# Three expert slots at 96 tokens in unrounded float32, in two and four column tiles, in place of 128 tokens in split precision

## The chip, the cores and the metric

One core of one Trainium2 chip runs the whole program in one launch. The metric is the device time of that launch in microseconds (us), lower is better. Three runs of the kernel before gave 1510.27, 1510.45 and 1510.76 us, median 1510.45. TensorE is called PE here, its weight loads PEld, VectorE DVE, ScalarE ACT, GpSimd POOL, SyncE SP.

## What is computed

A two-layer encoder over 256 tokens of width 1024. Each layer has three mixing branches (a gated MLP, latent attention, differential attention), and then a feed-forward part: dense in layer 0, a mixture of experts in layer 1. Only the mixture is touched:

```python
def swiglu(h, w1, w3, w2):
    return (jax.nn.silu(h @ w1) * (h @ w3)) @ w2

def moe_ffn(h, router, w1, w3, w2):
    logits = (h @ router).astype(jnp.float32)
    top_v, top_i = lax.top_k(logits, TOP_K)          # 2 of 8
    top_w = jax.nn.softmax(top_v, axis=-1)
    gates = jnp.sum(jax.nn.one_hot(top_i, N_EXPERTS, dtype=jnp.float32) * top_w[..., None], axis=-2)
    y = gates[..., 0:1] * swiglu(h, w1[0], w3[0], w2[0])
    for e in range(1, N_EXPERTS):
        y = y + gates[..., e:e + 1] * swiglu(h, w1[e], w3[e], w2[e])
    return y
```

There are 8 experts, each with w1 and w3 of 1024x3584 and w2 of 3584x1024 in float32, 44 MB an expert. Evaluated with its own inputs, the reference's router sends 38 tokens to expert 0 and 97, 73, 45, 64, 66, 54 and 75 to experts 1 to 7 (512 places in all).

## The kernel before

**Stages.** Layer 0, layer 1's mixer, the router, and then the experts, one *slot* after the other. SP loads each expert in 42 units of 1 MB (128 partitions x 2048 floats) into a ring of 14 buffers (`eraw`). It loads a unit as soon as the matmuls on the unit 14 places before it are done (`eunit_done`). PE works on the units in the order of the table `ORDER`, which for the four column blocks (`PAIRS`) of the hidden layer holds the units of w1, w3 and w2. A unit has two k-steps of 128 rows x 1024 columns; the four units of w1 and w3 of the last, half as wide block have four k-steps of 128 x 512. That makes 92 k-steps in a slot: 76 of 1024 columns and 16 of 512.

**Slots.** `PLAN = "WLWWL"` gives the kinds of slots 0 to 4. Slot 0 is always expert 0. Experts 1 to 7 are ranked by their number of tokens; the three with the fewest take the light slots (1, 4 and the last, 7), the others the wide ones. A slot that is needed because an expert has more tokens than its slot has room is put in behind slot 6.

- A *wide* slot (W, 128 tokens, function `slot`) works in split precision. ACT rounds the weights (`ehi <- eraw`, `unit_hi`), DVE makes the rest (`elo <- eraw, ehi`, `unit_lo`), and PE multiplies three times for each 512 columns: high by high (L2001), high weights by low tokens (L2002), low weights by high tokens (L2006).
- A *light* slot (L, 64 tokens, `light_slot`) multiplies the loaded float32 weights as they are (L2533). The stationary tokens are 64 wide, so PE's array is used as two column tiles: one matmul computes the left half of the columns for output partitions 0 to 63, the next one the right half for partitions 64 to 127. In the trace each such float32 matmul is two records.

**Around a slot.** After w1 and w3 of a block, ACT takes silu, DVE the product into `hid`, and PE transposes `hid` at fixed units (`TURNS`); at unit 31 PE also gathers the next slot's tokens. The reads of the units are waited for on `eraw_in`.

**Ahead of slot 0.** PE finishes the last mixer units (`token_pair`), with the transposes of the first 128 tokens in between (`tokens_turned(0)`), computes the router's logits with the router's 8 columns as the stationary operand (`logits`, L2205), transposes the second 128 tokens, computes their logits, and places the tokens (L2413 to L2417). DVE builds the selection matrix `Gm`; PE gathers expert 0's tokens with it (L2553), ACT and DVE split them (`hehi`, `helo`), and slot 0 begins.

Of the kernel before, what the change touches and what calls it, by code (L numbers as in the profile page):

```python
# [43 lines left out]


SLOT = P
EXTRA = 2 * TOKENS // (SLOT + 1)
SLOTS = NE + EXTRA
MORE = -(-TOKENS // SLOT) - 1
NM = NE * MORE  # L50
assert MORE == 1

PLAN = "WLWWL"
LIGHT, CAP = PLAN.count("L") + 1, 64
RANKED = NE - 1
LOOP = len(PLAN)
assert PLAN[0] == "W"


def is_light(s):
    return PLAN[s] == "L"


def lights_before(s):
    return PLAN[:s].count("L")


def wides_before(s):  # L70

    return s - (lights_before(s) if isinstance(s, int) else LIGHT - 1)


def slot_row(s):

    if isinstance(s, int) and s < LOOP:
        if is_light(s):
            return SLOT + CAP * lights_before(s)
        return SLOT * wides_before(s) + (CAP * (LIGHT - 1) if s else 0)  # L80
    return s * SLOT - (SLOT - CAP) * (LIGHT - 1)
# [5 lines left out]
def rank_of_slot(s):  # L87
    return lights_before(s) if s < LOOP and is_light(s) else LIGHT + wides_before(s) - 1
# [80 lines left out]
T_LOW = T_IOTA + SLOT  # L169
T_THR = T_LOW + NE * NE  # L170
T_EID = T_THR + NM
T_TRIM = T_EID + NM
T_IDX = T_TRIM + NM * NM
T_COS = T_IDX + EXTRA
T_SIN = T_COS + NB * ROPE // 2
T_W = T_SIN + NB * ROPE // 2
# [59 lines left out]
def encoder(nc, ins, out):  # L236
    ctx = ExitStack()
    with ctx:
# [46 lines left out]
        rt = keep("rt", [P, KD, NE])  # L285
# [98 lines left out]
        ea32 = at("ea32", over_mask, [P, 8, CAP])  # L384
        last32 = at("last32", over_xn + 4096, [P, 4, CAP])
# [3 lines left out]
        lgT = keep("lgT", [NE, TOKENS])  # L389
# [16 lines left out]
        qm = keep("qm", [P, NB, NE])  # L406
        tmp = keep("tmp", [P, EXTRA, NM])
        tmp2 = keep("tmp2", [P, 2, NB, EXTRA, NM])
# [12 lines left out]
        he32 = keep("he32", [P, KD, CAP])  # L421
# [106 lines left out]
        first_hehi = sem("first_hehi")  # L528
# [42 lines left out]
        xs_all = nc.dram_tensor("xs_all", [slot_row(SLOTS) + SLOT, D], F32, kind="Internal")  # L571
# [59 lines left out]
        def light_tiles(p):  # L631

            return last32 if p == PAIRS - 1 else ea32

# [76 lines left out]
        def _(pool):  # L711
# [31 lines left out]
            pool.dma_start(rt[:, :, :], ins["moe_router"][0].rearrange("(k p) e -> p k e", p=P)).then_inc(router_in, 16)  # L743
# [21 lines left out]
            for i in range(TABLE_BLOCKS):  # L765
                pool.wait_ge(unit_done, MIX_UNITS + 6 + 3 * i // 2)
                r = min(SLOT * i, slot_row(SLOTS))
                pool.dma_start(xs_all[r:r + SLOT, :], zeros[:, :]).then_inc(zeroed, 16)
# [22 lines left out]
            def slot_in(s):  # L791
                if isinstance(s, int) and s in DIRECT:
                    return
                n = CAP if isinstance(s, int) and s < LOOP and is_light(s) else SLOT
                pool.dma_start(xs[0:n, :], xs_all[bass.ds(slot_row(s), n), :]).then_inc(xs_in, 16)
# [20 lines left out]
            for s in range(1, LOOP + 1):  # L816
                result_waited(s)
                if not is_light(s - 1):
# [5 lines left out]
                pool.wait_ge(y_left, 16 * lights_before(s))  # L824
# [38 lines left out]
        def turned_place(b, k):  # L863

            return small[:, 2 * b + k // 4, P * (k % 4):P * (k % 4) + P]

        def first_place(k):
# [3 lines left out]
            return t[:, SLOT * (k % 2):SLOT * (k % 2) + SLOT]  # L873

# [9 lines left out]
        def _(act):  # L884
# [233 lines left out]
            def outputs(s):  # L1118

                act.wait_ge(eunit_done, UNITS * s + UNITS)  # L1120
                if isinstance(s, int) and is_light(s):
                    act.activation(ysb[:, 0:512], small[:, 0, :], ACT.Copy).then_inc(y_ready, 1)
# [9 lines left out]
            def slot(s, first=False):  # L1132
                for n in range(UNITS):
# [6 lines left out]
                    if first and n == 5:  # L1140

                        act.wait_ge(lmax_ready, 1)
                        for b in range(NB):
                            i = act.activation(ex[:, b, :], lg[:, b, :], ACT.Exp, bias=lmax[:, b:b + 1],
                                               scale=nrs[:, 3, b:b + 1])
                        i.then_inc(lexp_ready, 1)
# [20 lines left out]
                    if n == GATES_TURNED + 2 and first:  # L1167

                        act.wait_ge(gt_done, 1)
                        act.activation(GT[:, :, :].rearrange("j b t -> j (b t)"), small[0:SLOT, 2, 0:NB * P],  # L1170
                                       ACT.Copy).then_inc(gt_ready, 1)
                    if n in HE_TAKEN and not (isinstance(s, int) and is_light(s + 1)):
# [4 lines left out]
            def light_slot(s, i, final=False):  # L1177
                for n in range(UNITS):
                    if n == 3:
# [3 lines left out]
                    for p in range(PAIRS):  # L1183
                        if n == unit_end(p, 0):

                            act.wait_ge(eunit_done, UNITS * s + n + 1)
                            if p:
                                act.wait_ge(light_turned, PAIRS * i + p)
                            act.activation(hid[:, 0:light_width(p)], big[0][:, 0, 0:light_width(p)],
                                           ACT.Silu).then_inc(sil_done, 1)  # L1190
                        if n == TURNS[2 * p]:

                            act.wait_ge(light_turned, PAIRS * i + p + 1)
                            tiles = light_width(p) // P
                            src = small[:, turn_bank(2 * p), 0:2 * tiles * CAP].rearrange("p (j h t) -> p j h t", j=tiles, h=2)
                            dst = light_tiles(p)[:, 0:2 * tiles, :].rearrange("p (h j) t -> p j h t", h=2)
                            act.activation(dst, src, ACT.Copy).then_inc(light_taken, 1)
                    if n in HE_TAKEN and not final and not (s + 1 < LOOP and is_light(s + 1)):
# [7 lines left out]
            unit_hi(0, 0)  # L1206
# [5 lines left out]
            def squares(b):  # L1212
                for half in range(2):
                    act.wait_ge(x_ready, 8 + 2 * b + half + 1)
                    part = slice(512 * half, 512 * half + 512)
                    i = act.activation(xn[:, b, part], X[:, b, part], ACT.Square, accum_out=nss[:, 3, half, b:b + 1])
                return i

            def tokens_taken(b):
                act.wait_ge(norm_turned, 12 + 2 * b + 1)  # L1220
                for k in range(4):
# [3 lines left out]
            squares(0)  # L1225
            tokens_taken(0)
            tokens_taken(1)
            squares(1).then_inc(ss_ready, 1)
            act.wait_ge(var_ready, 4)
            act.activation(nsd[:, 3, :], nvar[:, 3, :], ACT.Sqrt, scale=1.0 / D, bias=eps[:, :]).then_inc(sd_ready, 1)  # L1230
            act.wait_ge(unit_done, NU - 2)
            unit_hi(0, 1)
# [4 lines left out]
            for k in range(KD):  # L1237
                act.wait_ge(first_gather, k // 2 + 1)
                a = act.activation(hehi[:, k, :], first_place(k), ACT.Copy, scale=pcol[:, G_ROUTE + k:G_ROUTE + k + 1])
                if k % 2:  # L1240
                    a.then_inc(first_hehi, 1)
            slot(0, first=True)
            for s in range(1, LOOP):
                if is_light(s):
                    light_slot(s, lights_before(s))
# [6 lines left out]
            light_slot(last, LIGHT - 1, final=True)  # L1252
# [27 lines left out]
        def _(dve):  # L1280
# [125 lines left out]
            def mixer(l):  # L1406
# [220 lines left out]
                if l:  # L1627
# [6 lines left out]
                    dve.memset(room[:, 0:1], float(SLOT))  # L1634
# [14 lines left out]
                def tokens_taken(b):  # L1649
                    dve.wait_ge(norm_turned, 12 + 2 * b + 2)  # L1650
                    for k in range(4, KD):
# [9 lines left out]
                else:  # L1661

                    unit_lo(0, 0)
# [3 lines left out]
                    tokens_taken(0)  # L1667
                    add(1, G_O + 1)
                    tokens_taken(1)
# [51 lines left out]
            dve.tensor_copy(lgT[:, :], big[0][0:NE, 0, 0:TOKENS]).then_inc(lgt_ready, 1)  # L1721
# [19 lines left out]
            own(dve.tensor_scalar(qS[:, :, 0:NE], pos[:, :, :], -1.0, None, ALU.add))  # L1741
# [3 lines left out]
            def picked():  # L1745

                for b in range(NB):
                    i = dve.tensor_scalar(Gm[:, b, :], iota, qS[:, b, 0:1], nrs[:, 3, b:b + 1], ALU.is_equal, ALU.mult)
                i.then_inc(g_ready, 1)

# [15 lines left out]
            def gathered(s, i):  # L1766

                dve.wait_ge(hehi_ready, 2 * (wides_before(s) - 1) + i + 1)
# [17 lines left out]
            def ranked():  # L1786
# [11 lines left out]
                dve.tensor_scalar(room[:, 1:NE], place_of[:, :], float(LIGHT), float(CAP - SLOT), ALU.is_lt, ALU.mult)  # L1798
# [9 lines left out]
            def extra_slots():  # L1808


                own(dve.tensor_tensor(need[:, :], counts[:, :], room[:, :], ALU.is_gt))
# [17 lines left out]
            def extra_places():  # L1829
                for b in range(NB):  # L1830
                    i = dve.tensor_tensor(qm[:, b, :], qS[:, b, 0:NE], room[:, :], ALU.subtract)
                own(i)
                for j, part in enumerate((qm[:, :, :], gS[:, :, 0:NE])):
                    for b in range(NB):
                        i = dve.tensor_tensor(tmp2[:, j, b, :, :], pick[:, :, :], bc(part[:, b, :], 1, [P, EXTRA, NM]), ALU.mult)
                own(i)
                dve.tensor_reduce(qS[:, :, NE:SLOTS], tmp2[:, 0, :, :, :], AX.X, ALU.add)
                own(dve.tensor_reduce(gS[:, :, NE:SLOTS], tmp2[:, 1, :, :, :], AX.X, ALU.add))
                dve.tensor_copy(metai[:, :], meta[:, :]).then_inc(routed, 1)

            def destinations():
# [8 lines left out]
                dve.tensor_scalar(shift[:, :], idx[:, :], float(SLOT), float(slot_row(NE - 1)), ALU.mult, ALU.add)  # L1850
# [5 lines left out]
                own(dve.tensor_tensor(over[:, :, :], over[:, :, :], placed[:, :, :], ALU.add))  # L1856
                for c in range(2):
# [11 lines left out]
            unit_lo(0, 1)  # L1869
# [782 lines left out]
```

## Time and profile before

| | us |
|---|---|
| median of three runs | 1510.45 |
| the profiled execution | 1509.97 |
| its span, first to last instruction | 1508.3 |
| slot 0 (W), first matmul to that of slot 1 | 119.45 |
| slot 1 (L), to the first matmul of slot 2 | 81.94 |
| slot 2 (W) | 119.93 |
| slot 3 (W) | 118.46 |
| slot 4 (L) | 82.45 |

TensorE's granted clock is 0.999 of 2.4 GHz over the span. In a profile, a record of PE has its start and a modelled end; matmuls overlap, so the pace of the engine is the distance from start to start, not the length of a record.

### The profile page before, as it was taken

Reading aid. Unit: us, or ns where it says so; the run is one execution under the profiler, and the core shown is the slowest. Engines: PE = TensorE matmul, PEld = TensorE weight load, DVE = VectorE, ACT = ScalarE, POOL = GpSimd, SP = SyncE. Lnnn points to the kernel's source line nnn. Section 1 sums busy time; section 2 is a strip of 40 time slices with the busy share of each in tenths; the row PEclk is TensorE's granted clock in tenths of the full one; section 3 lists DMA queues with packets and bytes.
Section 4 is the critical chain, followed back from the end, with each engine's and each line's share of the span. In section 5 each row is a group of like instructions: output and inputs, shape, how many; then the busy total and the mean of one; then the engine's idle time right before and its main releaser. Section 6 shows DMA issues by size and latency. Waiting matters only on the chain.

```text
span 1508.3 us, 19634 instructions
## 1 busy us (share of the span) xinstructions
PE 1481.6 (98%) x7704; PEld 1146.8 (76%) x7704; DVE 967.4 (64%) x899; ACT 794.3 (53%) x787; POOL 98.2 (7%) x101
## 2 busy tenths in 40 slices
PE   9999999999999999999999999999999999999996
PEld 8888889999898888878853588888734688888532
DVE  6856776455467667689930399898700798998301
ACT  5465635343354655487720387777501786877201
POOL 2000000000000000002000000200000000200041
PEclk9999999999999999999999999999999999999999
DMA  9555455778575554899999999999999999999996
GB/s 338 197 168 175 147 186 177 232 257 249 186 256 168 168 171 151 325 389 382 406 390 427 426 427 427 424 421 427 390 411 427 427 426 427 427 428 408 388 426 282
DMA packets 111772, 488.65 MB, mean 324 GB/s; under 512 B 8492, under 2 KB 12720, under 8 KB 68688
## 3 DMA queue, kind: packets, MB, share of 16 engines
q1 hardware_dynamic: 103520, 459.58, 78.3%
q0 software_dynamic: 7600, 27.37, 4.9%
q8 instruction: 57, 0.93, 0.2%
q10 hardware_dynamic: 576, 0.61, 0.1%
q14 instruction: 19, 0.16, 0.0%
HBM read 473.37 MB, written 15.21 MB: 324 GB/s over the span
## 4 chain that ended last, share of the span: by engine, by line
PE 87%; DMA 6%; DVE 3%; SPq 2%; ACT 2%; issue 1%; DVEq 0%; ACTq 0%
PE big L2001 15%; PE big L2006 15%; PE big L2002 14%; PE big L2533 7%; DMA eraw<-experts 6%; PE small L2006 6%; PE small L2001 5%; PE small L2002 5%; PE big L2078 4%; PE big L2085 4%; PE big L2079 4%; PE small L2106 3%; SPq L696 2%; DVE elo L1393 2%; PE small L2533 1%; ACT ehi L1108 1%
## 5 line engine op out<-in xcount | busy, mean ns | idle before, releaser
L1393 DVE TENSOR_TENSOR elo<-eraw,ehi 128x2048 fp32r<-128x2048 f32 x210 | 476.0, 2289 | 69.9 <-ACT ehi L1108 68.1
L1108 ACT ACTIVATE ehi<-eraw 128x2048 fp32r<-128x2048 f32 x210 | 401.3, 1919 | 149.3 <-PE big L2006 64.4
L1297 DVE TENSOR_TENSOR wlo<-raw,whi 128x2048 fp32r<-128x2048 f32 (+2 forms) x104 | 229.9, 2217 | 140.9 <-ACT whi L895 140.0
L895 ACT ACTIVATE whi<-raw 128x2048 fp32r<-128x2048 f32 (+2 forms) x103 | 190.6, 1857 | 223.3 <-PE big L2006 83.3
L2001 PE MATMUL big<-ehi,hehi 128*128 128x512 f32 x560 | 219.9, 393 | 5.3 <-ACT ehi L1108 5.2
L2002 PE MATMUL big<-ehi,helo 128*128 128x512 f32 x560 | 218.1, 389 | 0.0
L2001 PE MATMUL big<-whi,hhi 128*128 128x512 f32 (+1 forms) x384 | 151.9, 396 | 0.0
L2006 PE MATMUL big<-elo,hehi 128*128 128x512 f32 x560 | 150.3, 390 | 0.8 <-DVE elo L1393 0.8
L2533 PE MATMUL big<-eraw,he 128*64 128x512 f32 (+1 forms) x768 | 147.6, 541 | 2.7 <-DMA eraw<-experts 2.7
L2002 PE MATMUL big<-whi,hlo 128*128 128x512 f32 (+1 forms) x384 | 149.0, 388 | 0.0
L1952 DVE TENSOR_TENSOR hid<-hid,big 128x512 f32<-128x512 f32 (+1 forms) x12 | 7.5, 622 | 206.6 <-PE big L2533 206.6
L2001 PEld LDWEIGHTS big<-ehi,hehi 128*128 128x128 f32 x560 | 105.2, 188 | 29.2 <-ACT ehi L1108 4.6
L2006 PEld LDWEIGHTS big<-elo,hehi 128*128 128x128 f32 x560 | 104.8, 188 | 24.2 <-DVE elo L1393 2.5
L2533 PEld LDWEIGHTS big<-eraw,he 128*64 128x64 f32 x768 | 54.0, 137 | 89.4 <-issue 80.7
L2002 PEld LDWEIGHTS big<-ehi,helo 128*128 128x128 f32 x560 | 105.2, 188 | 21.3
L2078 PE MATMUL big<-hhi,whi 128*128 128x256 f32 x480 | 117.4, 285 | 0.9 <-DVE hlo L1307 0.7
L2079 PE MATMUL big<-hlo,whi 128*128 128x256 f32 x480 | 116.7, 283 | 0.0
L2006 PE MATMUL big<-wlo,hhi 128*128 128x512 f32 (+1 forms) x384 | 94.9, 387 | 0.0
L2001 PE MATMUL small<-ehi,eahi 128*128 128x512 f32 x240 | 94.0, 391 | 0.0
L2078 PEld LDWEIGHTS big<-hhi,whi 128*128 128x128 f32 x480 | 92.0, 192 | 1.9 <-issue 1.1
L2002 PE MATMUL small<-ehi,ealo 128*128 128x512 f32 x240 | 93.4, 389 | 0.0
L2079 PEld LDWEIGHTS big<-hlo,whi 128*128 128x128 f32 x480 | 92.1, 192 | 0.2
(405 smaller groups left out, 1855.7 us busy)
## 6 DMA issues: line engine op xcount, KB each, us to landing
eraw<-experts SPq DMA_DIRECT2D x336, 1024.0 KB, 16.9
raw<-ffn_w SPq DMA_DIRECT2D x30, 1024.0 KB, 5.8
raw<-w_gate SPq DMA_DIRECT2D x24, 1024.0 KB, 5.0
raw<-w_in SPq DMA_DIRECT2D x19, 1024.0 KB, 5.1
raw<-w_branch SPq DMA_DIRECT2D x12, 1024.0 KB, 5.0
raw<-w_o SPq DMA_DIRECT2D x8, 1024.0 KB, 5.0
xs_all<-zeros POOLq DMA_DIRECT2D x11, 512.0 KB, 7.0
raw<-w_in SPq DMA_DIRECT2D x4, 896.0 KB, 9.2
```

The costliest lines, as they stand in the source:

```text
L895: act.activation(whi[u % HI][:, 0:kt, 0:cols], raw[u % RAW][:, 0:kt, 0:cols], ACT.Copy).then_inc(hi_ready, 1)
L1108: act.activation(ehi[HI_OF[n]][:, :], eraw[n % RING][:, :], ACT.Copy).then_inc(ehi_ready, 1)
L1297: dve.tensor_tensor(wlo[u % RAW][:, 0:kt, 0:cols], raw[u % RAW][:, 0:kt, 0:cols], whi[u % HI][:, 0:kt, 0:cols].bitcast(F32), ALU.subtract) ...
L1393: dve.tensor_tensor(elo[n % RING][:, :], eraw[n % RING][:, :], ehi[HI_OF[n]][:, :].bitcast(F32), ALU.subtract).then_inc(elo_ready, 1)
L2001: pe.matmul(o, sh, mh, start=start, stop=False, **kw)
L2002: return pe.matmul(o, sl, mh, start=False, stop=False, **kw)
L2006: return pe.matmul(o, sh, ml, start=False, stop=stop, **kw)
L2078: pe.matmul(place(n), w_of, ahi[:, k0 + k, :], start=start, stop=False, skip_group_check=True)
L2079: pe.matmul(place(n), w_of, alo[:, k0 + k, :], start=False, stop=False, skip_group_check=True)
L2085: i = pe.matmul(place(n), wlo[u % RAW][:, k, n * P:n * P + P], ahi[:, k0 + k, :], start=False, stop=last and k == kt - 1, skip_group_check ...
L2106: return pe.transpose(o, src, ident[0:n, 0:n])
L2533: d = pe.matmul(out[CAP * side:CAP * side + CAP, 0:cols], x32[:, t, :], raw32[:, k, cols * side:cols * side + cols], start=start, stop=stop)
```

## The change

`PLAN` becomes `"MLMML"`. A *medium* slot (M) has room for 96 tokens and works on unrounded float32 as a light slot does: tokens 0 to 63 in two column tiles of 64, as before, and after them, in the same k-step, tokens 64 to 95 in four column tiles of 32, each with a quarter of the columns. Slots 0, 2 and 3 are medium; expert 0 takes slot 0, and of the ranked experts the fourth and fifth lightest take slots 2 and 3. The two fullest take the wide slots 5 and 6. Slots 1, 4 and the last stay light. In M slots ACT's and DVE's conversions of the weights (`unit_hi`, `unit_lo`) are gone, and so is the split of the tokens; silu and product work on 768 columns instead of 1024 (128 partitions). A medium slot writes its result in six transfers instead of one.

```diff
-PLAN = "WLWWL"
-LIGHT, CAP = PLAN.count("L") + 1, 64
+PLAN = "MLMML"
+CAP, MID = 64, 96
+LIGHT = PLAN.count("L") + 1
+MEDIUM = PLAN[1:].count("M")
...
                     def products(k, stop):
                         t = tiles * q + k
                         start = t == 0 and (m < 2 or p == 0)
+                        shared = medium and cols < 512
                         for side in range(2):
-                            d = pe.matmul(out[CAP * side:CAP * side + CAP, 0:cols], x32[:, t, :],
-                                          raw32[:, k, cols * side:cols * side + cols], start=start, stop=stop)
+                            d = pe.matmul(out[CAP * side:CAP * side + CAP, 0:cols], x32[:, t, 0:CAP],
+                                          raw32[:, k, cols * side:cols * side + cols], start=start, stop=stop, skip_group_check=shared)
+                        if medium:
+                            w = cols // 2
+                            for j in range(TILES):
+                                d = pe.matmul(out[COLS * j:COLS * j + COLS, cols:cols + w], x32[:, t, CAP:MID],
+                                              raw32[:, k, w * j:w * j + w], start=start and not shared, stop=stop,
+                                              skip_group_check=shared)
                         return d
...
                             for j in range(w // P):
                                 d = turn(small[:, turn_bank(2 * p), P * j:P * j + P], hid[:, P * j:P * j + P])
+                            if medium:
+                                at = 0 if p < PAIRS - 1 else w
+                                for j in range(w // P // 2):
+                                    d = turn(small[:, 3, at + P * j:at + P * j + P], hid[:, w + P * j:w + P * j + P])
```

The router is changed too. Its matrix is padded to 32 columns and its eight products rotate over four column tiles; the four partial sums are added by the small matmul that had been the transpose of `lgT`. Half of the second 128 tokens are transposed inside the last mixer unit, and their read-out is shared out anew between ACT and DVE:

```diff
-                    i = pe.matmul(big[0][0:NE, 0, P * b:P * b + P], rt[:, k, :], hT[:, k, P * b:P * b + P], start=k == 0,
-                                  stop=k == KD - 1)
+                    rows = slice(COLS * (k % TILES), COLS * (k % TILES) + COLS)
+                    i = pe.matmul(big[0][rows, 0, P * b:P * b + P], rt[:, k, :], hT[:, k, P * b:P * b + P], start=k < TILES,
+                                  stop=k >= KD - TILES)
...
-            logits(0)
-            tokens_turned(1)
-            logits(1).then_inc(logits_done, 1)
+            logits(0, range(KD))
+            logits(1, range(4))
+            tokens_turned(1, (range(4, KD),))
+            logits(1, range(4, KD)).then_inc(logits_done, 1)
```

On PE, ahead of slot 0, from the last mixer product to the first matmul of the token placement, there stood before (rows read: line, operation, output<-inputs, stationary columns x moving columns, count):

```order
L2006 MATMUL big<-wlo_78,hhi 128x512 x4
L2205 MATMUL big<-hT,rt 8x128 x8
L2106 MATMUL small<-tab,X 128x128 x8
L2205 MATMUL big<-hT,rt 8x128 x8
L2123 MATMUL small<-tab 128x128
L2106 MATMUL small<-tab,lgT 128x8 x2
```

and there stands now (the first row is the first half of the transposes, ahead of the last four products of the mixer):

```order
L2166 MATMUL small<-tab,X 128x128 x4
L2064 MATMUL big<-wlo_78,hhi 128x512 x4
L2269 MATMUL big<-hT,rt 32x128 x12
L2166 MATMUL small<-tab,X 128x128 x4
L2269 MATMUL big<-hT,rt 32x128 x4
L2183 MATMUL small<-tab 128x128
L2473 MATMUL small<-tab,lgT 128x8 x2
```

Four of the eight transposes moved ahead of the mixer's last products, and four of the second tokens' eight products moved ahead of the other four transposes.

On PE, the first unit of slot 0 and what is ahead of it, before (L2553 is the gather, `he` the tokens, `eraw_142` the first ring buffer):

```order
L2553 MATMUL big<-Gm,X 128x128 x4
L2001 MATMUL big<-ehi_138,hehi 128x512
L2002 MATMUL big<-ehi_138,helo 128x512
L2001 MATMUL big<-ehi_138,hehi 128x512
L2002 MATMUL big<-ehi_138,helo 128x512
L2001 MATMUL big<-ehi_138,hehi 128x512
L2002 MATMUL big<-ehi_138,helo 128x512
L2001 MATMUL big<-ehi_138,hehi 128x512
L2002 MATMUL big<-ehi_138,helo 128x512
L2006 MATMUL big<-elo_156,hehi 128x512 x4
```

and now, with the second unit behind it:

```order
L2649 MATMUL big<-Gm,X 128x96 x4
L2609 MATMUL big<-eraw_142,he_179 64x512 x2
L2614 MATMUL big<-eraw_142,he_179 32x256 x4
L2609 MATMUL big<-eraw_142,he_179 64x512 x2
L2614 MATMUL big<-eraw_142,he_179 32x256 x4
L2609 MATMUL big<-eraw_143,he_179 64x512 x2
L2614 MATMUL big<-eraw_143,he_179 32x256 x4
L2609 MATMUL big<-eraw_143,he_179 64x512 x2
L2614 MATMUL big<-eraw_143,he_179 32x256 x4
```

A unit of 12 matmuls, all 128 wide, became one of 12 float32 matmuls whose width goes from 64 to 32 and back in each k-step.

## Rows read from the trace of the kernel before

**Rows 1.** The page: busy times, granted clock by slice, chain that ended last.

```profile
PE 1481.6 (98%) x7704; PEld 1146.8 (76%) x7704; DVE 967.4 (64%) x899; ACT 794.3 (53%) x787; POOL 98.2 (7%) x101
...
PEclk9999999999999999999999999999999999999999
...
PE 87%; DMA 6%; DVE 3%; SPq 2%; ACT 2%; issue 1%; DVEq 0%; ACTq 0%
```

**Rows 2.** Windows, slots 0 to 4: length, busy us, PEclk, DMA share, GB/s.

```profile
652.05:771.50 119.45, 119.23 (x547) 98.08 (x547) 109.16 (x125) 86.05 (x59) 14.20 (x9) 1.00 0.97 387
771.50:853.44 81.94, 79.01 (x416) 31.02 (x415) 4.76 (x13) 9.36 (x18) 1.55 (x4) 1.00 1.01 420
853.44:973.37 119.93, 119.33 (x541) 98.22 (x542) 107.60 (x63) 90.89 (x63) 7.37 (x4) 1.00 1.01 426
973.37:1091.83 118.46, 118.46 (x543) 97.98 (x543) 102.34 (x58) 83.53 (x52) 6.79 (x5) 1.00 1.00 412
1091.83:1174.28 82.45, 79.04 (x415) 31.01 (x415) 4.67 (x13) 9.36 (x18) 1.51 (x4) 1.00 1.00 419
```

**Rows 3.** PE's timeline in slot 1: around the first transposes of `hid`, and w3's units.

```profile
788.65 1.89 PE L2533 MATMUL big<-eraw,he 128*64 128x512 f32 x8
790.47 0.66 PE L2106 MATMUL small<-tab,hid 128*128 128x128 f32 x4
791.05 1.94 PE L2533 MATMUL big<-eraw,he 128*64 128x512 f32 x8
...
816.73 4.46 PE L2533 MATMUL big<-eraw,he 128*64 128x512 f32 x20
```

**Rows 4.** PE's timeline in slot 1, later transposes, and the gather behind them.

```profile
827.99 0.66 PE L2106 MATMUL small<-tab,hid 128*128 128x128 f32 x4
828.48 2.73 PE L2498 MATMUL big<-Gm,X 128*128 128x128 f32 x23
```

**Rows 5.** PE's timeline in slot 1, units with 256 moving columns.

```profile
832.15 7.13 PE L2533 MATMUL big<-eraw,he 128*64 128x256 f32 x64
```

**Rows 6.** PE's timeline, from the last mixer products into the router.

```profile
637.51 0.39 PE L2002 MATMUL big<-whi,hlo 128*128 128x512 f32 x1
637.74 1.08 PE L2006 MATMUL big<-wlo,hhi 128*128 128x512 f32 x4
638.75 1.91 PE L2205 MATMUL big<-hT,rt 128*8 128x128 f32 x16
640.60 1.09 PE L2106 MATMUL small<-tab,X 128*128 128x128 f32 x8
```

**Rows 7.** The timeline of all engines, router to first gather.

```profile
638.86 0.69 DVE L1647 TENSOR_TENSOR X<-X,big 128x512 f32<-128x512 f32 x1 [1.64 <-PE big L2006]
...
641.71 2.04 PE L2205 MATMUL big<-hT,rt 128*8 128x128 f32 x16
641.73 1.13 DVE L1652 TENSOR_SCALAR hT<-small,pcol 128x128 f32<-128x128 f32 x4 [2.18 <-PE small L2106]
...
643.78 0.41 DVE L1721 COPY lgT<-big 8x256 f32<-8x256 f32 x1
...
647.59 0.17 DVE L1741 TENSOR_SCALAR qS<-pos 128x16 f32<-128x16 f32 x1
```

**Rows 8.** PE's timeline, first gather and first matmul of slot 0.

```profile
651.24 1.06 PE L2553 MATMUL big<-Gm,X 128*128 128x128 f32 x8
652.05 0.47 PE L2001 MATMUL big<-ehi,hehi 128*128 128x512 f32 x1
```

**Rows 9.** PE's timeline, from slot 1 into slot 2.

```profile
849.04 1.94 PE L2533 MATMUL small<-eraw,last 128*64 128x512 f32 x8 [0.48 <-DMA eraw<-experts]
853.44 0.47 PE L2001 MATMUL big<-ehi,hehi 128*128 128x512 f32 x1 [2.46 <-ACT ehi L1108]
```

**Rows 10.** The chain that ended last, from slot 1 into slot 2.

```profile
825.94 29.17 DMA eraw<-experts
855.13 1.92 ACT ehi L1108
857.08 2.30 DVE elo L1393
```

**Rows 11.** PE's timeline, the last unit of slot 4.

```profile
1169.78 1.94 PE L2533 MATMUL small<-eraw,last 128*64 128x512 f32 x8 [0.56 <-DMA eraw<-experts]
```

**Rows 12.** DMA issues: operation and count, KB each, median us to landing.

```profile
eraw<-experts SPq DMA_DIRECT2D x336, 1024.0 KB, 16.9
```

More of the change, by code:

```diff
@@ L633, in light_tiles, with native_width @@
             return last32 if p == PAIRS - 1 else ea32
+        def native_width(p, medium):
+            return light_width(p) * 3 // 2 if medium else light_width(p)
         def light_width(p):
@@ L1140, in slot @@
                     if first and n == 5:
[L1142 to L1146, printed above, removed]
+                        expert_weights()
                     if not first or n >= EARLY:
@@ L1235, in _ @@
                 act.activation(xn[:, b, :], X[:, b, :], ACT.Copy, scale=nrs[:, 3, b:b + 1]).then_inc(xn_ready[b], 1)
[L1237 to L1242, printed above, removed]
+            light_slot(0, 0, first=True)
             for s in range(1, LOOP):
-                if is_light(s):
-                    light_slot(s, lights_before(s))
+                if is_native(s):
+                    light_slot(s, natives_before(s))
                 else:
@@ L1827, in extra_slots, with slots_known @@
                                       float(slot_row(SLOTS) - SLOT * SLOTS), ALU.mult, ALU.add))
[L1829 to L1838, printed above, removed]
+            def slots_known():
                 dve.tensor_copy(metai[:, :], meta[:, :]).then_inc(routed, 1)
@@ L1958, in light_slot @@
                         (light_gathered if to_light else gathered)(s + 1, HE_TAKEN.index(n))
-            slot(0, first=True)
+            light_slot(0, first=True)
             for s in range(1, LOOP):
-                (light_slot if is_light(s) else slot)(s)
+                (light_slot if is_native(s) else slot)(s)
             dve.wait_ge(routed, 1)
@@ L2052, in token_pair @@
                                       whi[u % HI][:, k, 0:cols], False)
+                        if b and half:
+                            late()
                         pe.wait_ge(lo_ready, u + 1)
@@ L2487, in slot @@
                     if n == GATHERED:
-                        gather(s + 1, CAP if isinstance(s, int) and is_light(s + 1) else SLOT)
+                        gather(s + 1, capacity(s + 1) if isinstance(s, int) else SLOT)
             def gather(s, rows):
@@ L2506, in gather, with gates_turned, light_slot @@
                     i.then_inc(gather_done, 1)
-            def light_slot(s, i, final=False):
+            def gates_turned():
+                pe.wait_ge(gg_ready, 1)
+                for b in range(NB):
+                    i = turn(small[0:SLOT, 2, b * P:b * P + P], Gg[:, b, :])
+                i.then_inc(gt_done, 1)
+            def light_slot(s, i, final=False, first=False):
+                medium = not final and is_medium(s)
                 for n in range(UNITS):
                     p, m, q = ORDER[n]
-                    if n == 0:
+                    if first and n < 4:
+                        pe.wait_ge(first_he, n + 1)
+                    elif n == 0:
                         pe.wait_ge(he_ready, 2 * s)
@@ L2539, in light_slot @@
                     d.then_inc(eunit_done, 1)
+                    if n == GATES_TURNED and first:
+                        pe.wait_ge(light_taken, 2)
+                        gates_turned()
                     for p in range(PAIRS):
```

326 lines of the change are left out of this document (196 added, 130 removed).

## The prediction

> **What bounds the kernel now.** I read the page first: PE is busy 98% of the span at full clock and makes up 87% of the chain that ended last [rows 1]. Then the windows by slot. In the three wide slots that change, PE is busy 119.23 of 119.45, 119.33 of 119.93 and 118.46 of 118.46 us; DVE (102 to 109 us) and ACT (84 to 91 us) are close behind but do not hold it. At the same time the DMA engines are at a share of 0.97 to 1.01 and move 387 to 426 GB/s [rows 2]. So there are two bounds near each other, PE in wide slots and the loads in light ones: slot 1 ends with PE waiting for a landing [rows 9], and the chain holds a piece of 29.17 us that is a load [rows 10]. What the change is worth is decided by one question: how long PE needs for a medium slot, against some 119 us.
>
> **Pace of PE in float32.** I read it from spans of many records, not from record lengths. In slot 1 twenty records, ten passes of the tile pair, span 4.46 us and eight span 1.89 [rows 3]: six passes more in 2.57, so a pass takes 0.43 us for 512 columns (0.429), both tiles of a pair run side by side in it, and the last one ends 0.60 after its start. With 256 columns 64 records (32 passes) span 7.13, so a pass takes 0.215 us [rows 5]. Transposes with 128 columns follow each other at 0.11 [rows 4, 6]. So a pass costs its columns at 0.84 ns each, and a float32 matmul is two passes.
>
> **A k-step of a medium slot.** 64 tokens: two passes of 512, 0.86 us. 32 tokens: the four tiles each take 256 columns; if they run side by side as the pairs do, two passes of 256, 0.43 us. Together 1.29; in the half-wide block 0.645. A slot has 76 of the first and 16 of the second: 97.9 + 10.3 = 108.2 us. To this come the transposes, 6 + 6 + 6 + 3 of `hid` and 8 of the gather at 0.11, 3.2 us. Without anything else a medium slot would be some 111.4 us, 7 below a wide one. It has the same number of column passes as the wide one and gains only in pace.
>
> **The change of tile width.** This is the term that decides. In rows 3 the four passes that start at 788.65 are streamed at 788.65 + 4 x 0.429 = 790.37, but the first 128-wide transpose starts at 790.47, 0.10 later; then four transposes span 0.66 where 3 x 0.11 + 0.27 = 0.60 would do, 0.05 more. Going back, the transposes are streamed at 790.96 and the 64-wide matmul starts at 791.05, 0.09 later, and its eight records span 1.94 instead of 1.89, another 0.05. So a change of width costs 0.15 us to 128 and 0.145 us to 64. It is not the transposes and not the wait in front of them: transposes followed by a 128-wide gather start 0.49 us apart for four, at their usual pace with no gap behind [rows 4]. The router shows it a third time: the four 128-wide products, 0.23 apart, are streamed at 637.74 + 4 x 0.23 = 638.66, and the 8-wide matmul starts at 638.75, some 0.10 later with nothing more behind (16 records in 1.91 = 15 x 0.109 + 0.27, the length of a single one); on the way back 0.10 and 0.05 [rows 6].
>
> A medium slot changes width twice in each of its 92 k-steps, from 64 to 32 and back. No row shows that very change. Its bounds are 0 (the gap belongs only to changes between the whole array and tiles) and 0.15 each. I take the rows' value, as all four directions that the trace has show at least 0.10: 0.145 to 64, and to 32 between the 0.10 of 8 columns and the 0.145 of 64, 0.115. That is 0.26 per k-step, S below. The Trainium skill ("TensorEngine Tiling (Array Packing)", Tiling Modes, Key Properties) says that changing the tiling mode, not just the tile, drains TensorE, and lists 128x64 and 128x32 as different modes; by it the rows' gap would be paid here too, 92 times two. The trace agrees for 128 to 64, 128 to 8 and back. A sum that counted only passes, as that page's speedup table does, would give 1490 instead of the figure below.
>
> So M = 108.2 + 3.2 + 92 x 0.26 + 0.6 (each of the four groups of transposes adds one change) = **135.9 us** for a medium slot; in general 112.0 + 92 S.
>
> **The sum.**
> - *Start of slot 0.* Today the X half lands at 639.55 (DVE, 638.86 + 0.69), but PE first does 16 router records and transposes from 640.60; the second products start at 641.71 and DVE copies the logits at 643.78 [rows 6, 7]. Afterwards four transposes (0.45) come earlier and delay the half to 640.0; meanwhile twelve products run in four tiles, 3 x 2 passes of 0.11, 0.65 us. The other four transposes take 0.6, read-out two per engine 0.28 each (four in 1.13) with about 0.2 to start, then one group of four products, 0.5 with its tail: copy at about 641.8, 2.0 earlier. The step on `qS` (0.17) moves behind `Gm` [rows 7]. I take 2.2 us; the gather still ends it [rows 8]. Bounds 0 and 3.
> - *Slot 0:* -2.2 + 135.9 - 119.45 = **+14.3** [rows 2].
> - *Slot 1* stays: same code, starts with a full ring.
> - *Slot 2:* slot 1's last unit is done at about 849.04 + 1.94 = 850.98 [rows 9]; today slot 2 is through at 973.37, 122.39 later, since its first units go from landing over ACT and DVE to PE [rows 9, 10]. A medium slot starts on the landed unit; its second lands at 855.11 (825.94 + 29.17), so it is held by about 1.0. 1.0 + 135.9 - 122.39 = **+14.5**.
> - *Slot 3:* 135.9 - 118.46 = **+17.4** [rows 2].
> - *Slots 4 to 7* stay: slot 4 starts with a full ring as today.
> - *At nothing:* ACT and DVE conversions of three slots, up to 109 us of DVE a slot. They lay beside PE's work; their absence shortens nothing but the start of slot 2. The 768-column silu and product and the second read-out of transposes fall on engines that are now nearly idle, with two or more units of PE's work between a transpose and its use. The six result transfers instead of one are on POOL, and the copy that waits for them comes a slot later. DMA: fewer bytes per us are asked for than today, so it is no bound in M slots.
>
> Sum +46.2. The profiled execution took 1509.97 (span 1508.3, 1.7 around it), 0.5 below the median of the runs: **1556 us**.
>
> **What would decide it otherwise.** The total is 3 M - 361.5, zero at M = 120.5, S = 0.092, 46 ns a change. With S = 0.20 (0.10 each) it is +29.7, 1540; with S = 0.30 +57.3, 1567.
>
> **Rivals.**
> 1. *Changes between 64 and 32 cost nothing; faster.* For it: the rows only show changes that include 128 or an 8-wide tile. Against it: the 8-wide matmul is also a tile of the array, and it paid both ways [rows 6]. Then M = 112.6 (108.2 + 3.2 + four groups of transposes at 0.29). Slot 0 gives -2.2 - 6.9 = -9.0. Slots 2 and 3 would give -8.8 - 5.9 = -14.7, but now the loads bind: slots 2 to 4 need 126 units, at 426 GB/s 2.46 us each for 1.049 MB [rows 2, 12], 310.1 us, and took 320.7 (850.98 to 1171.72) [rows 9, 11], so at most -10.6. Sum -19.6: **1490**. It decides from 46 ns a change downward. Chance 0.20, with 0.03 for a partial cost that ends within 0.2% (S about 0.08 to 0.10) and 0.02 for one that ends between 1490 and 1507.
> 2. *The four tiles of 32 don't run side by side*, four float32 streams at once being more than any row shows (pairs at most). Then the 32 tokens cost 4 x 0.43 instead of 0.43 a k-step: 76 x 1.29 + 16 x 0.645 = 108 us more a slot, about **1880**. The Trainium skill ("TensorE: Matmul & The Clock Gate", Part 3) gives 2.38 times for three column tiles of 32 and some 4 ns for each further tile; no run here shows it. Chance 0.04.
> 3. *A ninth slot*, some 118 us [rows 2], if 96 are too few for an expert in an M slot: excluded by the counts, 38 for expert 0 and 66 and 73 for the fourth and fifth lightest; the loads show that today's 8 slots (336 units of 42) suffice [rows 12].
>
> **How the numbers follow.** Width changes paid as in the rows: 0.71, of which its own range is 1540 to 1567. Serial tiles 0.04, faster 0.22, within 0.2% 0.03. 0.2% (3 us) is about what a measurement of this kernel can tell from no change. The range must take in the faster case, else it leaves out more than 0.2: 1487 to 1569, the bounds of the two large cases with 2 or 3 us for the start. Chances: faster 0.22, same 0.03, slower 0.75.
>
> **What the profile after would show.** PE in a medium slot: passes of 0.43 and 0.215, and between the last 32-wide pass and the next 64-wide record 0.09 to 0.10 of gap, with 0.05 more behind it, in each of 92 k-steps. Slot 0 some 136 long and starting near 649.9; slots 2 and 3 136 to 137; slots 1 and 4 still near 82; in M slots the loads near 42 x 1.049 MB in 136 us, 324 GB/s, with the queue waiting for PE. If instead k-steps start every 1.29 us, rival 1 holds and light slots get longer; if the four 32-wide records start 0.2 apart, rival 2. ACT and DVE should be idle for most of M slots without anyone gaining.

## The result, and the profile after

The changed kernel takes 1566.28 us (median of 4 runs, 1566.0 to 1567.3), the kernel before beside it 1510.36 (1509.29 to 1510.76). The ratio is 1.0373, 95% interval 1.0361 to 1.0386: slower by 55.9 us, where 46 was forecast. The profiled execution took 1567.3 us with a span of 1565.7, 57.4 above the span before.

The page after, its lines of busy times and of the chain (against [rows 1]):

```profile
PE 1539.7 (98%) x9485; PEld 959.4 (61%) x9485; DVE 665.8 (43%) x735; ACT 547.5 (35%) x642; POOL 87.7 (6%) x120
...
PE 91%; DMA 6%; SPq 1%; ACT 1%; DVE 1%; issue 0%; DVEq 0%; ACTq 0%
```

DVE and ACT lost 302 and 247 us of work, and PE's work did not get shorter for it. Windows of the profile after, slots 0 to 4 (columns as in [rows 2]; slot 1 and slot 4 end here with their last matmul):

```profile
652.41:791.28 138.87, 138.87 (x1136) 35.65 (x1136) 15.06 (x76) 6.76 (x14) 5.32 (x9) 1.00 0.92 340
791.28:872.08 80.80, 79.08 (x418) 31.06 (x414) 3.41 (x6) 5.17 (x9) 4.05 (x9) 1.00 1.01 414
872.08:1011.09 139.01, 138.52 (x1133) 35.63 (x1133) 4.35 (x6) 6.69 (x13) 2.00 (x5) 1.00 0.99 404
1011.09:1149.59 138.50, 138.50 (x1137) 35.46 (x1133) 4.93 (x10) 6.90 (x13) 3.43 (x8) 1.00 0.89 322
1149.59:1228.26 78.67, 78.67 (x418) 31.03 (x414) 4.64 (x12) 7.23 (x17) 3.99 (x9) 1.00 1.00 419
```

A medium slot takes 138.5 to 139.0 us where a wide one took 118.5 to 119.9 [rows 2], with PE busy throughout, and the loads fall to 322 GB/s once they only follow PE. Why it is that long stands in PE's timeline in slot 0, two k-steps:

```profile
700.57 1.08 PE L2609 MATMUL big<-eraw,he 128*64 128x512 f32 x4
701.58 0.64 PE L2614 MATMUL big<-eraw,he 128*32 128x256 f32 x8
702.15 1.08 PE L2609 MATMUL big<-eraw,he 128*64 128x512 f32 x4
703.16 0.64 PE L2614 MATMUL big<-eraw,he 128*32 128x256 f32 x8
```

A k-step is 702.15 - 700.57 = 1.58 us, where its passes are 1.29. From 64 to 32 wide the start is 1.01 away, for 0.86 of passes; from 32 to 64 it is 0.57, for 0.43. So the pair of changes costs 0.29. The eight 32-wide records span 0.64: two passes of 0.215 and the tail, so four tiles do run side by side (one after the other, eight records would take 1.7).

Where the 57.4 us of span came from, slot by slot (slot 0 from its first matmul, a light slot to its last):

| | before | after | difference | forecast |
|---|---|---|---|---|
| first matmul of slot 0 | 652.05 | 652.41 | +0.4 | -2.2 |
| slot 0 | 119.45 | 138.87 | +19.4 | +16.5 |
| slot 1 | 79.48 | 80.80 | +1.3 | 0 |
| slot 2, from the end of slot 1 | 122.39 | 139.01 | +16.6 | +14.5 |
| slot 3 | 118.46 | 138.50 | +20.0 | +17.4 |
| slot 4 | 79.87 | 78.67 | -1.2 | 0 |
| the rest | | | +0.8 | 0 |

### The profile page after: what moved, and what is told of

Same layout as the page of the kernel before. It is cut to its first block, busy times and chain, and to the rows that moved or that the text cites. A ratio compares the mean times of both kernels' runs of the same rounds, so it can differ in the third digit from the quotient of the medians.

```text
span 1565.7 us, 22782 instructions
## 1 busy us (share of the span) xinstructions
PE 1539.7 (98%) x9485; PEld 959.4 (61%) x9485; DVE 665.8 (43%) x735; ACT 547.5 (35%) x642; POOL 87.7 (6%) x120
## 3 DMA queue, kind: packets, MB, share of 16 engines
q8 instruction: 71, 1.16, 0.3%
## 4 chain that ended last, share of the span: by engine, by line
PE 91%; DMA 6%; SPq 1%; ACT 1%; DVE 1%; issue 0%; DVEq 0%; ACTq 0%
PE big L2609 18%; PE big L2059 10%; PE big L2060 10%; PE big L2064 10%; PE small L2609 7%; PE big L2614 6%; DMA eraw<-experts 5%; PE big L2138 4%; PE big L2145 4%; PE big L2139 4%; PE small L2614 3%; PE small L2059 3%; PE small L2060 3%; PE small L2064 3%; PE small L2166 3%; SPq L720 1%
## 5 line engine op out<-in xcount | busy, mean ns | idle before, releaser
L2609 PE MATMUL big<-eraw,he 128*64 128x512 f32 (+1 forms) x1536 | 334.3, 553 | 3.1 <-DMA eraw<-experts 3.1
L930 ACT ACTIVATE whi<-raw 128x2048 fp32r<-128x2048 f32 (+2 forms) x103 | 190.6, 1857 | 225.9 <-PE big L2064 79.9
L1439 DVE TENSOR_TENSOR elo<-eraw,ehi 128x2048 fp32r<-128x2048 f32 x84 | 190.7, 2289 | 30.9 <-ACT ehi L1143 30.1
L2609 PEld LDWEIGHTS big<-eraw,he 128*64 128x64 f32 x1536 | 92.0, 136 | 157.1 <-issue 148.4
L1143 ACT ACTIVATE ehi<-eraw 128x2048 fp32r<-128x2048 f32 x84 | 160.9, 1920 | 61.2 <-PE big L2064 25.8
L2609 PE MATMUL small<-eraw,ea 128*64 128x512 f32 x576 | 142.8, 606 | 3.4 <-DMA eraw<-experts 3.3
L2614 PE MATMUL big<-eraw,he 128*32 128x256 f32 (+1 forms) x1536 | 112.5, 364 | 0.0
L2059 PE MATMUL big<-ehi,hehi 128*128 128x512 f32 x224 | 88.5, 395 | 2.5 <-ACT ehi L1143 2.5
L2060 PE MATMUL big<-ehi,helo 128*128 128x512 f32 x224 | 88.1, 393 | 0.0
L2059 PEld LDWEIGHTS big<-whi,hhi 128*128 128x128 f32 x384 | 72.1, 188 | 16.9 <-issue 3.3
L2060 PEld LDWEIGHTS big<-whi,hlo 128*128 128x128 f32 x384 | 72.2, 188 | 14.1 <-issue 0.5
```

Of the source, the lines that this page charges most:

```text
L930: act.activation(whi[u % HI][:, 0:kt, 0:cols], raw[u % RAW][:, 0:kt, 0:cols], ACT.Copy).then_inc(hi_ready, 1)
L1143: act.activation(ehi[HI_OF[n]][:, :], eraw[n % RING][:, :], ACT.Copy).then_inc(ehi_ready, 1)
L1439: dve.tensor_tensor(elo[n % RING][:, :], eraw[n % RING][:, :], ehi[HI_OF[n]][:, :].bitcast(F32), ALU.subtract).then_inc(elo_ready, 1)
L2059: pe.matmul(o, sh, mh, start=start, stop=False, **kw)
L2060: return pe.matmul(o, sl, mh, start=False, stop=False, **kw)
L2609: d = pe.matmul(out[CAP * side:CAP * side + CAP, 0:cols], x32[:, t, 0:CAP], raw32[:, k, cols * side:cols * side + cols], start=start, stop ...
```

## The experiments

The kernel before was run beside each group of them, at medians of 1510.95, 1510.21 and 1509.89 us. Ratios are to it.

**1. Fewer width changes, same work** (`e1_unit`, `e2_snake`, `e3_snake2`). The two widths of a k-step become two passes over a unit (`part(n, width)` does all its k-steps at one width); then units alternate which width comes first; then groups of two units do so:

```diff
...
-                    for k in range(tiles):
-                        d = products(k, k == tiles - 1 and (n == UNITS - 1 or (m < 2 and tiles * q + k == KD - 1)))
-                    d.then_inc(eunit_done, 1)
...
+                        if not SNAKE or any(ORDER[n][0] == PAIRS - 1 and ORDER[n][1] < 2 and ORDER[n][2] == 0 for n in ns):
+                            width = CAP
+                        for n in ns:
+                            arrive(n)
+                            part(n, width)
+                        width = CAP + COLS - width
+                        for n in ns:
+                            part(n, width).then_inc(eunit_done, 1)
...
```

> Same work as the changed kernel, but in a medium slot the 64-wide matmuls of all k-steps of a unit come first and then the 32-wide ones: 42 pairs of width changes in a slot instead of 92. Theory (a width change costs 0.1455 us, half of the 0.291 per k-step read in the changed kernel): 50 x 0.291 = 14.6 us less per medium slot, slot about 124.3, total about 1522.6. Rival A (the 32-wide matmuls themselves are slow, however they are ordered): no change, 1566. Rival B (loads or waits hold the slot): no change either.

> As the one before, but every second unit starts with the width at which the last one ended, so that a unit has one width change: 42 changes in a slot instead of 184. Theory: 142 x 0.1455 = 20.7 us less per medium slot than in the changed kernel, slot about 118, total about 1504, which is below the kernel before. Rival A: 1566.

> As the one before, but in groups of two units: 22 width changes in a slot. Theory: 162 x 0.1455 = 23.6 us less per medium slot than in the changed kernel, slot about 115.2, total about 1496. Rival A: 1566. Rival C (once PE is this fast, the loads hold the end of slot 4): 1 to 5 us above that, seen as waits for landings in slot 4.

Measured: 1523.11 us (1.0084, 1.0067 to 1.0101), 1508.29 (0.9984, 0.9975 to 0.9994) and 1508.17 (0.9984, 0.9974 to 0.9993). The order of the same matmuls is worth 58 us, so rivals A and B of the expectations are out. Slot 3 of each, from the windows of the three profiles in this order:

```profile
982.78:1106.86 124.08, 124.08 (x1137) 44.57 (x1134) 4.93 (x10) 6.90 (x13) 3.42 (x8) 1.00 0.98 385
```

```profile
970.90:1089.52 118.62, 118.62 (x1135) 48.15 (x1133) 4.93 (x10) 6.91 (x13) 3.43 (x8) 1.00 1.01 416
```

```profile
968.38:1084.12 115.74, 115.74 (x1135) 50.05 (x1133) 4.94 (x10) 6.80 (x13) 3.43 (x8) 1.00 1.01 425
```

With 184, 84, 42 and 22 changes between 64 and 32 the slot takes 138.5, 124.1, 118.6 and 115.7 us, PE busy in all of it: 0.144, 0.131 and 0.145 us a change from one to the next. The uneven step comes from what is not counted: where the width is the same on both sides of a group of 128-wide transposes, the group adds two changes and not one. Counted in the order of `ORDER` and `TURNS` with those changes in, a slot has 187, 87, 50 and 30, and the price is 0.144, 0.148 and 0.144. On to none, 115.7 - 30 x 0.145 = 111.4, what passes and transposes alone add up to in the prediction (108.2 + 3.2). The slots came out as the theory says (124.3, 118, 115.2), and so did the first total (1522.6). The other two totals are 4 and 12 us above it. In the windows of the third, the light slots are 83.3 long, where the kernel before has 79.5 and 79.9:

```profile
767.47:850.72 83.25, 79.58 (x416) 31.10 (x412) 3.42 (x6) 5.17 (x9) 4.05 (x9) 1.00 1.01 418
...
1084.12:1167.41 83.29, 80.04 (x416) 31.05 (x412) 4.64 (x12) 7.23 (x17) 3.99 (x9) 1.00 1.01 423
```

and PE's timeline at the end of its slot 4 shows the last units of w2 waited for one by one, and then slot 5's first weights:

```profile
1158.16 1.94 PE L2614 MATMUL small<-eraw,ea 128*64 128x512 f32 x8 [0.19 <-DMA eraw<-experts]
1160.60 1.94 PE L2614 MATMUL small<-eraw,ea 128*64 128x512 f32 x8 [0.51 <-DMA eraw<-experts]
1163.02 1.94 PE L2614 MATMUL small<-eraw,last 128*64 128x512 f32 x8 [0.48 <-DMA eraw<-experts]
1165.47 1.94 PE L2614 MATMUL small<-eraw,last 128*64 128x512 f32 x8 [0.52 <-DMA eraw<-experts]
1170.67 0.80 PE L2060 MATMUL big<-ehi,hehi 128*128 128x512 f32 x1 [3.27 <-ACT ehi L1144]
```

**2. Half of each load left out** (`e8_snake2_half`), to see whether that is the whole of it:

```diff
-                    sp.dma_start(eraw[n % RING][:, :], src).then_inc(eraw_in[n % RING], 16)
+                    part = slice(0, 1024 if half or (first and n >= RING) else 2048)
+                    sp.dma_start(eraw[n % RING][:, part], src[:, part]).then_inc(eraw_in[n % RING], 16)
```

> The kernel with 22 width changes in a medium slot (groups of two units, 1508.2 us where 1496 was expected), with half of each unit's load left out in slots 0 to 4 once the ring is full (those experts compute with stale halves). If the loads took back the missing 12 us: slots 1 and 4 fall to 78.7 (from 83.3 both), slots 0, 2 and 3 stay at 115.5 to 116.3, and slot 5 starts without waiting for a landing, total about 1491. If PE itself (wrongly priced width changes) is the cause: unchanged, 1508.

Measured: 1490.81 us (0.9872, 0.9852 to 0.9892). Its windows:

```profile
652.27:768.77 116.50, 116.50 (x1137) 50.43 (x1137) 15.07 (x76) 6.66 (x14) 5.32 (x9) 1.00 0.66 220
768.77:847.19 78.42, 78.42 (x417) 31.16 (x415) 3.42 (x6) 5.16 (x9) 4.04 (x9) 1.00 0.85 282
847.19:962.96 115.77, 115.77 (x1136) 50.19 (x1134) 4.35 (x6) 6.58 (x13) 1.99 (x5) 1.00 0.61 202
962.96:1078.70 115.74, 115.74 (x1135) 50.05 (x1133) 4.93 (x10) 6.80 (x13) 3.42 (x8) 1.00 0.60 195
1078.70:1157.25 78.55, 78.55 (x417) 31.01 (x413) 6.02 (x13) 10.55 (x19) 3.98 (x9) 1.00 0.92 331
```

The medium slots keep their PE time (slot 2 is without its 1.4 us of waits), the light slots are at 78.4 and 78.6, and PE waits for nothing in these five slots. So full loads cost the kernel of 22 changes 17 us: 11.3 in slots 0 to 4, the rest behind them, where slot 5's start waits 3.3 us in the one kernel and not in the other. That is more than the 12 us missed above, since the kernel before waits for loads too (at the ends of its light slots and the starts of slots 2 and 5 [rows 9, 11]); how much it would gain from half loads was not measured.

**3. No width change in the k-steps** (`e5_all32`). All 96 tokens go into 32-wide tiles, three groups a k-step, and the hidden layer's and the results' layout follow (light slots keep their products):

```diff
...
-                        for side in range(2):
-                            d = pe.matmul(out[CAP * side:CAP * side + CAP, 0:cols], x32[:, t, 0:CAP],
-                                          raw32[:, k, cols * side:cols * side + cols], start=start, stop=stop, skip_group_check=shared)
-                        if medium:
-                            w = cols // 2
...
+                        w = cols // 2
+                        for g in range(MID // COLS):
                             for j in range(TILES):
-                                d = pe.matmul(out[COLS * j:COLS * j + COLS, cols:cols + w], x32[:, t, CAP:MID],
-                                              raw32[:, k, w * j:w * j + w], start=start and not shared, stop=stop,
-                                              skip_group_check=shared)
+                                d = pe.matmul(out[COLS * j:COLS * j + COLS, w * g:w * g + w], x32[:, t, COLS * g:COLS * g + COLS],
+                                              raw32[:, k, w * j:w * j + w], start=start and w * g % 512 == 0, stop=stop,
+                                              skip_group_check=True)
...
```

> Medium slots with all 96 tokens in four column tiles of 32, three groups a k-step: the same passes as in the changed kernel and no width change except around the transposes. Theory (only passes and width changes cost PE anything): 1.29 us a k-step, a slot of about 112.5 us. For the total two theories differ. PE alone decides: three slots at 112.5 give about 1490. The loads hold the light slots (in the two runs with few width changes the last unit of slot 3 landed at the same 1060.7 us as in the kernel before): slot 4 cannot end before some 1164, total about 1503. Rival (24 matmuls a k-step, four float32 streams at once, are more than PE can be fed with): a slot well over 113.

Measured: 1510.58 us (0.9999, 0.999 to 1.0008), as the kernel before; neither 1490 nor 1503. Its slots 0, 2 and 3 take 116.88, 118.30 and 118.28, not 112.5. In PE's timeline of slot 2 the passes keep their pace, and between them stand gaps that no semaphore ended; in slot 3 the 128 records behind such a gap span 5.37 us instead of 3.70, of which more below:

```profile
939.79 3.68 PE L2621 MATMUL big<-eraw,he 128*32 128x128 f32 x128
944.95 3.70 PE L2621 MATMUL big<-eraw,he 128*32 128x128 f32 x128 [1.48 <-issue]
950.88 1.74 PE L2621 MATMUL big<-eraw,he 128*32 128x128 f32 x56 [2.24 <-issue]
...
1065.16 5.37 PE L2621 MATMUL big<-eraw,he 128*32 128x128 f32 x128 [2.22 <-issue]
1071.22 5.39 PE L2621 MATMUL small<-eraw,ea 128*32 128x256 f32 x96 [0.69 <-issue]
```

The view of PE's waits for slots 0 to 3 sums them:

```profile
PE big L2621 <- issue: 8.3, 5, 2.2
PE small L2615 <- DMA eraw<-experts: 2.3, 2, 1.1
PE small L2621 <- issue: 0.9, 2, 0.7
PE big L2621 <- DMA eraw<-experts: 0.5, 1, 0.5
```

Of the gaps without a releaser, 9.2 us in seven, the five of the first row (8.3) stand in the half-wide block, whose k-steps of 0.645 us have 12 matmuls, which are 24 records, with as many weight loads (the 24 of the expectation are records). The other two stand right behind that block.

**4. The same with half of each load left out** (`e7_half`, the edit of 2 on the kernel of 3).

> As the one before, but the loads of slots 0 to 4 bring only half of each unit once the ring has been filled (the other half is stale data, so these experts compute something else; passes, waits and order stay). If the loads hold the kernel before it, light slots fall to their PE time of 78.7, slot 4 ends near 1146 and the total is about 1485, some 18 us below its sibling with full loads. If PE alone decides there, the two are equal.

Measured: 1484.76 us (0.9839, 0.9824 to 0.9854). Slots 0, 2 and 3 now take 113.88, 113.03 and 114.30, and the view of PE's waits for the same stretch has one row:

```profile
PE small L2624 <- issue: 1.0, 1, 1.0
```

So full loads cost this kernel 26 us. By the windows of both kernels 12.3 of them stand in the three medium slots, 8.2 of which are gaps without a releaser; 7.6 stand in the light slots 1 and 4 (81.34 and 83.49 us against 78.57 and 78.62), and 6 behind slot 4. The rival of experiment 3, that PE can't be fed, holds beside full loads; with half of them three slots of 113.0 to 114.3 are near the 112.5.

**5. Slot 0 alone medium** (`e4_slot0`, `e4b_slot0`): `PLAN = "MLWWL"`.

> The changed kernel with its slots 2 and 3 wide again, slot 0 and the router as changed (one part alone). Theory (a medium slot costs its length, nothing is carried to other slots): the changed kernel less the 16.6 and 20.1 us that its slots 2 and 3 lost, 1529.6, with slot 0 at 138.9. Rival (medium slots disturb their neighbours): off from that by more than 2 us.

Measured: 1884.53 us. The plan was at fault, not the theory: with no medium slot behind slot 0 the changed kernel's formula takes 64 and then 32 off the 128 of a light expert's room, which leaves 32 tokens for experts that have 45, 54 and 64. Three more slots ran, as the page's issues show, 11 x 42 loads:

```profile
eraw<-experts SPq DMA_DIRECT2D x462, 1024.0 KB, 11.0
```

Each took 118.6 us, and 1529.6 + 3 x 118.6 is 1885. With the room mended:

```diff
-                dve.tensor_scalar(room[:, 1:NE], place_of[:, :], float(LIGHT), float(CAP - MID if MEDIUM else CAP - SLOT), ALU.is_lt,
+                dve.tensor_scalar(room[:, 1:NE], place_of[:, :], float(LIGHT), float(CAP - MID), ALU.is_lt,
```

> Slot 0 medium and slots 2 and 3 wide, with the rooms of the light experts computed rightly for that plan (8 slots). Theory: the changed kernel less what its slots 2 and 3 lost, 1566.3 - 16.6 - 20.1 = 1529.6, slot 0 at 138.9, slots 2 and 3 at 122 and 118.5 as in the kernel before.

Measured: 1527.54 us (1.0123, 1.0107 to 1.0138); slot 0 138.86, slots 2 and 3 121.63 and 118.39. A medium slot's loss stays in its slot. The total is 2.1 us below the forecast, just beyond the 2 us that the first expectation gave its rival: slot 0 starts at 651.09 here, 1.3 earlier than in the changed kernel's profile, and slots 1 and 2 take 200.3 us together where the kernel before took 201.9, so if slot 0 disturbs its neighbours, it is not by slowing them.

**6. The router alone** (`e6_router`): the kernel before with the second diff of the change and what goes with it.

> The kernel before with the change to the router alone (four column tiles, moved transposes, four partial sums). In the changed kernel the last mixer product and the first matmul of slot 0 are 11.73 us apart where they were 13.62, and 0.45 of transposes moved ahead of that product, so theory: 1.4 us less, total 1509.0, at the edge of what can be measured. Rival (the router gives the 2.2 us that were predicted): 1508.2. Rival (ACT and DVE, which still convert units here, hold slot 0's start anyway): 1510.4.

Measured: 1508.96 us (0.9996, 0.9987 to 1.0005). The median is where the theory has it, but the interval holds 1, so the total does not tell the rivals apart. Its profile does, in PE's timeline:

```profile
639.27 0.60 PE L2116 MATMUL small<-tab,X 128*128 128x128 f32 x4
639.63 1.18 PE L2014 MATMUL big<-wlo,hhi 128*128 128x512 f32 x4
640.74 0.86 PE L2219 MATMUL big<-hT,rt 128*32 128x128 f32 x24
641.58 0.66 PE L2116 MATMUL small<-tab,X 128*128 128x128 f32 x4
642.68 0.68 PE L2219 MATMUL big<-hT,rt 128*32 128x128 f32 x8 [0.44 <-DVE hT L1660]
...
652.22 0.47 PE L2009 MATMUL big<-ehi,hehi 128*128 128x512 f32 x1
```

From the mixer's last four products to slot 0 it is 12.59 us where it was 14.31 [rows 6, 8]; less the 0.36 of the four transposes ahead, 1.4 gained.

## Why the prediction was right

- **Width changes between 64 and 32 are paid.** Right, and the step on which all hung: no row before showed this change, the rows of four other directions were taken for it, and it costs what the dearest of them cost. The profile after shows it in each k-step, and experiment 1 removes it by order alone.
- **Its size** was the term that was mis-sized: 0.26 a pair was taken, 0.29 measured, near the upper bound of 0.30. That is 92 x 0.03 = 2.8 us a slot and 8 of the 10 us by which the forecast was short; 1566 lies just under the 1567 that the prediction gave for 0.30. The 32-wide side was put at 0.115, between the 8-column row and the 64-wide one; it costs 0.14 to 0.15, like the 64-wide one.
- **Passes** were right: 0.43 and 0.215, four tiles side by side, 111.4 us without any change in the sum, and 111.4 extrapolated in experiment 1. Rival 2 (serial tiles) is out.
- **Slots 1 and 4 stay** held within 1.3 us, and **slot 2's later start** too: the forecast's 1.0 of waiting was 0.49.
- **The start of slot 0** was forecast at -2.2 and came at +0.4. The router gave 1.8 from the mixer's last products on (12.51 from 639.90 to 652.41, where it was 14.31) and cost 0.35 ahead of them; the forecast had 2.65 less 0.45. The other 1.8 is from earlier: in this execution PE waits 1.12 us in layer 0's last dense step for a unit's conversion, which the execution before did not. The changed kernel has four more transfers of zeros, three of them shortly ahead of that wait, but of the nine other profiles three show a wait of 0.55 to 1.07 there and six none, so its cause stays open. PE's timeline of the changed kernel:

```profile
407.41 0.50 PE L2059 MATMUL small<-whi,fhi 128*128 128x512 f32 x1 [1.12 <-ACT whi L930]
...
639.90 1.18 PE L2064 MATMUL big<-wlo,hhi 128*128 128x512 f32 x4
...
652.41 1.08 PE L2609 MATMUL big<-eraw,he 128*64 128x512 f32 x4
```

- **Work that ACT and DVE lose is worth nothing** was right: 548 us less of it, and in the time only the 2.0 us by which slot 2 waits less for its first weights (0.49 against 2.46 [rows 9]), which the forecast had, at 1.0.
- **Rival 1's price was wrong**, though not its place. It gave 1490 for free changes: 9.0 us won up to the end of slot 0, kept, and 10.6 more from slot 2 to slot 4, where the loads would bind. Two of its terms failed. The 9.0 are not kept: slot 1 ends at 850.98 when slot 0 ends at 771.50 (before) and at 850.72 when slot 0 ends at 767.47 (22 changes), so the loads already hold the end of slot 1, and 0.3 is left. And the pace of the loads, taken as 2.46 us a unit, was 2.51: slots 2 to 4 took 316.7 us for 126 units, 4.0 less than before and not 10.6. The kernel with 22 changes ended at 1508.2 with loads and at 1490.8 with half of them. So had the changes been free, the kernel would, as an estimate from the kernels of 22 changes (1508.2) and of none (1510.6), have been about as fast as before or 0.2% faster, and not 1.3%; a medium slot had little to win here from the start. The range was wide for that case alone.

## What to carry to other kernels

When PE's tile width changes inside a loop, count the changes and give each a price from any such change in the trace (0.145 us here): the pair was a third of the 0.86 us of wide passes beside it, and ordering the same matmuls so that the width alternates once per unit and not twice per k-step was worth 58 us. Before costing an engine's gain, ask what the next bound leaves of it: the kernel of 22 changes ends at 1490.8 with half of its loads (experiment 2) and at 1508.2 with all, so 17 of the 75.5 us between the changed kernel and that bound went to the loads. The kernels of 42 and of 22 changes are both slightly faster than the kernel before (0.9984), so the better one is the simpler, with 42.

## What was not expected of the hardware

- **PE waited for its own instructions while the loads were at their limit.** The all-32 kernel has 29412 instructions against 22782, and its page shows 96 packets (1.57 MB) on the instruction queue against 71 (1.16 MB); with the loads at 421 GB/s PE stood idle 9.2 us in seven gaps with nothing to issue, with half loads 1.0 us in one.

```profile
q8 instruction: 96, 1.57, 0.4%
```

The DMA records of the two traces tie the gaps to this queue. Each of the eight gaps ends 1.3 to 1.6 us after a packet of 16 KB of the instruction queue has landed (one at 943.51 and PE's restart at 944.95, one at 949.51 and the restart at 950.88), and between two gaps of one slot PE does 127 or 128 matmul records with as many weight loads. How the loads hold it up is open: the transfer of a packet itself takes 0.94 us in the median with full loads and 0.95 with half.

- **The granted clock fell after idle time, though not each time.** In the kernel with 22 changes PE idles 3.27 us ahead of slot 5, and then runs at the lower of its two levels: the window 1170.70 to 1174.00 has a PEclk of 0.50 (1.2 of 2.4 GHz) and matmuls 0.43 apart, not 0.23. The kernel before idles 2.56 us there at full clock.

```profile
1170.70:1174.00 3.30, 3.30 (x8) 2.62 (x9) 2.71 (x2) 1.95 (x2) 0.00 (x0) 0.50 1.03 434
```

```profile
1174.28 0.50 PE L2001 MATMUL big<-ehi,hehi 128*128 128x512 f32 x1 [2.56 <-ACT ehi L1108]
```

The eleven profiles have twelve such waits for ACT of 2.4 to 3.3 us at the start of slot 2 or 5. With nine of them the clock went to half for 3.4 or 6.8 us about when PE went on, in the changed kernel too (idle for 2.49 us ahead of slot 5), with three it did not (2.46 and 2.56 us in the kernel before, 2.43 in the router's). The all-32 kernel has such a stretch of 3.4 us behind its gap of 2.22 us in slot 3, which is why the records at 1065.16 take 5.37 us, but none behind the gap of 2.24 in slot 2. What tells these apart isn't shown. In slot 5 it cost little: the slot takes 120.25 us in the changed kernel and 120.05 before. In the router's profile the 6.8 us lie at the start of slot 2, which takes 121.3 us and not 119.9; this execution took 1512.19 us, above its kernel's median of 1508.96.
